# Ten sums of squares totalled by two rounded products instead of one in plain fp32

## The reference

```python
h = _rmsnorm(x, g_mix[l])                      # norm 1: over 1024
p = h @ w_in[l]
c_q = _rmsnorm(p[..., :384], g_q[l])           # norm 3: over 384
c_kv = _rmsnorm(p[..., 384:640], g_kv[l])      # norm 2: over 256
# attention from c_q, c_kv and a roped key; a gated, 31 taps wide convolution u beside it
u = silu(_layernorm(u, g_conv_ln[l], b_conv_ln[l]))   # norm 4: variance over 512
x = x + concat([y_attn, u]) @ w_o[l]
h2 = _rmsnorm(x, g_ffn[l])                     # norm 5: over 1024
z = _dwconv(h2 @ w_up[l]); zg, zv = split(z)
x = x + (silu(zg) * zv) @ w_down[l]

def _rmsnorm(x, g):
    return x * rsqrt(mean(x * x, axis=-1) + EPS) * g
```

## Time and profile before

| | |
|---|---|
| median of 3 runs | 1915.56 us (1915.34 to 1915.62) |
| the profiled execution | 1915.41 us |
| its span | 1913.5 us |
| granted TensorE clock | 1.0 of full speed |
| TensorE busy | 1881.3 us, 98% of the span, 9081 matmuls |
| VectorE busy | 1147.8 us, 60% |
| ScalarE busy | 914.6 us, 48% |
| GpSimd busy | 80.8 us, 4% |
| DMA | 171.30 MB, mean 90 GB/s |

### The profile page before, as it was taken

The page is one execution under the profiler, slowest core; times in us unless marked ns, Lnnn a source line. Parts: engine busy times, 40 slices in busy tenths (PEclk is TensorE's granted clock), DMA queues, the critical chain, the costliest instruction groups (busy, mean ns, idle before and its releaser), DMA issues.

```text
span 1913.5 us, 27153 instructions
## 1 busy us (share of the span) xinstructions
PE 1881.3 (98%) x9081; PEld 1512.6 (79%) x9081; DVE 1147.8 (60%) x1954; ACT 914.6 (48%) x1675; POOL 80.8 (4%) x116
## 2 busy tenths in 40 slices
PE   8999999899999999999999999999999999999998
PEld 6888878788888877667888888888857888888887
DVE  6777675733333366677676667436568666666534
ACT  5666673534433344556543344334466554344433
POOL 2111000000000000100100000000010020000000
PEclk9999999999999999999999999999999999999999
DMA  4222223133333323530233332333541123333333
GB/s 146 74 66 71 78 80 108 61 110 99 94 99 97 95 67 86 121 67 29 83 100 103 94 99 91 102 99 86 120 86 45 56 80 108 99 94 93 96 96 104
DMA packets 169191, 171.30 MB, mean 90 GB/s; under 512 B 48546, under 2 KB 123280, under 8 KB 169104
## 3 DMA queue, kind: packets, MB, share of 16 engines
q1 hardware_dynamic: 169000, 170.14, 31.0%
q10 hardware_dynamic: 104, 0.03, 0.0%
HBM read 159.24 MB, written 2.10 MB: 84 GB/s over the span
## 4 chain that ended last, share of the span: by engine, by line
PE 87%; DVE 8%; ACT 3%; issue 1%; DMA 0%; SPq 0%; DVEq 0%; ACTq 0%
PE bank_b L2386 15%; PE bank_b L2388 15%; PE bank_b L2387 15%; PE bank_a L2386 12%; PE bank_a L2388 11%; PE bank_a L2387 11%; PE bank_b L2860 2%; PE bank_b L2963 1%; PE bank_a L2944 1%; DVE w_lo L1508 1%; DVE arena L1511 1%; DVE arena L1508 1%; DVE h_lo L1511 1%; DVE x_t L1508 1%; PE bank_a L2860 1%
## 5 line engine op out<-in xcount | busy, mean ns | idle before, releaser
L1508 DVE TENSOR_TENSOR w_lo<-w_raw,w_hi 128x512 fp32r<-128x512 f32 (+3 forms) x621 | 413.9, 679 | 572.3 <-ACT w_hi L1225 364.5
L1225 ACT ACTIVATE w_hi<-w_raw 128x512 fp32r<-128x512 f32 (+3 forms) x396 | 233.3, 599 | 437.6 <-PE bank_b L2388 224.8
L2386 PE MATMUL bank_b<-h_hi,w_hi 128*128 128x512 f32 (+1 forms) x952 | 373.7, 393 | 8.3 <-DVE w_lo L1508 6.7
L2388 PE MATMUL bank_b<-h_hi,w_lo 128*128 128x512 f32 (+1 forms) x952 | 369.3, 388 | 0.0
L2387 PE MATMUL bank_b<-h_lo,w_hi 128*128 128x512 f32 (+1 forms) x952 | 369.2, 388 | 0.0
L864 ACT ACTIVATE w_hi<-w_raw 128x512 fp32r<-128x512 f32 x225 | 137.5, 627 | 227.1 <-PE bank_b L2388 117.7
L2386 PE MATMUL bank_a<-h_hi,w_hi 128*128 128x512 f32 (+1 forms) x600 | 233.5, 389 | 3.9 <-DVE h_lo L1511 3.6
L2387 PE MATMUL bank_a<-h_lo,w_hi 128*128 128x512 f32 (+1 forms) x600 | 232.0, 387 | 0.0
L2388 PE MATMUL bank_a<-h_hi,w_lo 128*128 128x512 f32 (+1 forms) x600 | 231.9, 387 | 0.0
L2386 PEld LDWEIGHTS bank_b<-h_hi,w_hi 128*128 128x128 f32 x952 | 178.9, 188 | 49.5 <-DVE w_lo L1508 9.5
L2387 PEld LDWEIGHTS bank_b<-h_lo,w_hi 128*128 128x128 f32 x952 | 178.9, 188 | 36.7 <-issue 1.4
(11 more groups left out here) (294 smaller groups left out, 2557.7 us busy)
## 6 DMA issues: line engine op xcount, KB each, us to landing
w_raw<-in_w_up_dram SPq DMA_DIRECT2D x240, 256.0 KB, 3.1
w_raw<-in_w_down_dram SPq DMA_DIRECT2D x152, 256.0 KB, 2.6
arena<-arena SPq DMA_DIRECT2D x32, 268.0 KB, 4.0
w_raw<-in_w_in_dram SPq DMA_DIRECT2D x64, 128.0 KB, 2.3
w_raw<-in_w_gate_dram SPq DMA_DIRECT2D x32, 256.0 KB, 2.8
w_raw<-in_w_in_dram SPq DMA_DIRECT2D x32, 256.0 KB, 2.6
w_raw<-in_w_o_dram SPq DMA_DIRECT2D x32, 256.0 KB, 2.6
w_raw<-in_w_out_dram SPq DMA_DIRECT2D x16, 256.0 KB, 2.8
```

Of the source, the lines that this page charges most:

```text
L1225: nc.scalar.activation(w_hi[:, s, 0:c], w_raw[:, s, 0:c], ACT.Copy).then_inc(w_round, 1)
L1508: return nc.vector.tensor_tensor(out_, a, b, op)
L2386: nc.tensor.matmul(out_, a_hi, b_hi, start=start, stop=False, skip_group_check=loose)
L2388: return nc.tensor.matmul(out_, a_lo, b_hi, start=False, stop=stop, skip_group_check=loose)
```

## The change

The ten totals T1 to T5 of both layers are done otherwise. When the sum is complete, VectorE copies `ssum` into a rounded tile, and subtracts that from `ssum` into a second one (`split_sum`). TensorE multiplies both by `tri[:, 1, :]` and lets PSUM add them (`split_total`). The matrix holds minus ones, so the total comes with its sign turned, and the widths that divide it are negative. The two rounded tiles `ssum_r` take no room of their own: they lie over `var` and `rs0`. `ADDS` counts the additions with the two new steps per norm. The totals of the first block stay as they were.

```diff
+ADDS = [sum(tiles + 1 for tiles in (KT, KVT, QT, HT, KT)[:n]) for n in range(6)]
...
-    "sq_ready": (3 * KT, 2 * KT + QT + KVT + HT), "sq_added": (3 * (KT - 1) - 1, 2 * KT + QT + KVT + HT - 5),
+    "sq_ready": (3 * KT, 2 * KT + QT + KVT + HT), "sq_added": (3 * (KT - 1) - 1, ADDS[-1]),
...
         ssum = sb("ssum", [P, S])
+        with nc.sbuf_tensor("ssum_r", [P, 2, S], F32R) as ssum_r:
+            pass
         var = sb("var", [P, S])
         rs0 = sb("rs0", [P, S])
...
+            def split_sum(added):
+
+                dve.wait_ge(sq_added, added)
+                nc.vector.tensor_copy(ssum_r[:, 0, :], ssum[:, :]).then_inc(sq_added, 1)
+                dve.wait_ge(sq_added, added + 1)
+                rest(ssum_r[:, 1, :], ssum[:, :], ssum_r[:, 0, :]).then_inc(sq_added, 1)
...
# T1, before the memsets of the convolution's edges
+                split_sum(added0 + ADDS[1] - 2)
                 nc.vector.memset(upad[:, :, 0:HALO], 0.0).then_inc(pad_zero, 1)
...
-                rstd_of(norm0 + 1, bank_b[:, 3, :], 1)
+                rstd_of(norm0 + 1, bank_b[:, 3, :], 1, -D)
...
# T2, behind two products of the roped key
                 tt(rot[first, 1, :], krf[second, :], trig[second, :], ALU.mult).then_inc(kr_step, 1)
+                split_sum(added0 + ADDS[2] - 2)
                 split2_lo(M_Q + 4)
...
# T3
                     add_square(t, sq0 + KT + KVT, added0 + ADDS[2], was["stat_ready"] + 2)
+                split_sum(added0 + ADDS[3] - 2)
                 split2_lo(M_PAIR + 2)
...
# T4
                     add_square(j, sq0 + KT + KVT + QT, added0 + ADDS[3], norm0 + 3)
+                split_sum(added0 + ADDS[4] - 2)
                 for k in range(5, 8):
                     split2_lo(M_WO + k)
...
# T5
                 for k in range(KT):
                     split2_lo(M_UP + SLOTS + k)
+                    if k == 5:
+                        split_sum(added0 + ADDS[5] - 2)
...
+            def split_total(bank, added):
+
+                pe.wait_ge(sq_added, added)
+                nc.tensor.matmul(bank, tri[:, 1, :], ssum_r[:, 0, :], start=True, stop=False)
+                nc.tensor.matmul(bank, tri[:, 1, :], ssum_r[:, 1, :], start=False, stop=True).then_inc(stat_ready, 1)
...
-                            total(bank_b[:, 3, :], added0 + KT - 1)
+                            split_total(bank_b[:, 3, :], added0 + ADDS[1])
```

More of the change, by code:

```diff
@@ L832, in _ @@
                 sq0, added0 = was["sq_ready"], was["sq_added"]
-                pool.wait_ge(sq_added, added0 + KT - 1)
+                pool.wait_ge(sq_added, added0 + ADDS[1])
                 def diagonals(j):
@@ L846, in _ @@
                 diagonals(0)
-                add_squares(KVT, sq0 + KT, added0 + KT - 1, was["stat_ready"] + 1)
+                add_squares(KVT, sq0 + KT, added0 + ADDS[1], was["stat_ready"] + 1)
                 diagonals(1)
@@ L851, in _ @@
                 pool.wait_ge(stat_ready, was["stat_ready"] + 4)
-                add_squares(KT, sq0 + KT + KVT + QT + HT, added0 + KT + KVT + QT + HT - 4, was["stat_ready"] + 4)
+                add_squares(KT, sq0 + KT + KVT + QT + HT, added0 + ADDS[4], was["stat_ready"] + 4)
         @block.scalar
@@ L1271, in _ @@
                 for t in range(KVT):
-                    square(bank_a[:, t, :], t, sq0 + KT, added0 + KT - 1)
+                    square(bank_a[:, t, :], t, sq0 + KT, added0 + ADDS[1])
                 split2(M_Q + 4)
@@ L1317, in _ @@
                 split2(M_PAIR + 1)
-                act.wait_ge(sq_added, added0 + KT - 1 + KVT - 1)
+                act.wait_ge(sq_added, added0 + ADDS[1] + KVT - 1)
                 for t in range(QT):
                     act.wait_ge(lat_ready, was[lat_ready.name] + KVT + t + 1)
-                    square(bank_b[:, t, :], t, sq0 + KT + KVT, added0 + KT + KVT - 2)
+                    square(bank_b[:, t, :], t, sq0 + KT + KVT, added0 + ADDS[2])
                 split2(M_PAIR + 2)
@@ L1400, in _ @@
                     act.wait_ge(dev_ready, was[dev_ready.name] + j + 1)
-                    square(conv[:, j, :], j, sq0 + KT + KVT + QT, added0 + KT + KVT + QT - 3)
+                    square(conv[:, j, :], j, sq0 + KT + KVT + QT, added0 + ADDS[3])
                 for k in range(5, 8):
@@ L1427, in input_square @@
                 def input_square(turn):
-                    square(x_t[:, UP_ORDER[turn], :], turn, sq0 + KT + KVT + QT + HT, added0 + KT + KVT + QT + HT - 4)
+                    square(x_t[:, UP_ORDER[turn], :], turn, sq0 + KT + KVT + QT + HT, added0 + ADDS[4])
                 input_hi(0)
@@ L2151, in key_behind @@
                     rest(kr_lo[ND:P, :], rot[ND:P, 0, :], kr_hi[ND:P, :]).then_inc(kr_ready, 1)
-                rstd_after(norm0 + 2, bank_a[:, 3, :], KVL, key_behind)
+                rstd_after(norm0 + 2, bank_a[:, 3, :], -KVL, key_behind)
                 for t in range(KVT):
@@ L2170, in _ @@
                 for t in range(1, QT):
-                    add_square(t, sq0 + KT + KVT, added0 + KT + KVT - 2, was["stat_ready"] + 2)
+                    add_square(t, sq0 + KT + KVT, added0 + ADDS[2], was["stat_ready"] + 2)
+                split_sum(added0 + ADDS[3] - 2)
                 split2_lo(M_PAIR + 2)
                 split2_lo(M_PAIR + 3)
-                rstd_after(norm0 + 3, bank_b[:, 3, :], QL)
+                rstd_after(norm0 + 3, bank_b[:, 3, :], -QL)
                 tt(trig_q[0], trig[:, :], rstd[:, 0, :], ALU.mult).then_inc(trig_made, 1)
@@ L2271, in _ @@
                 for j in range(HT):
-                    add_square(j, sq0 + KT + KVT + QT, added0 + KT + KVT + QT - 3, norm0 + 3)
+                    add_square(j, sq0 + KT + KVT + QT, added0 + ADDS[3], norm0 + 3)
+                split_sum(added0 + ADDS[4] - 2)
                 for k in range(5, 8):
                     split2_lo(M_WO + k)
-                rstd_into(norm0 + 4, bank_b[:, 2, :], HALF)
+                rstd_into(norm0 + 4, bank_b[:, 2, :], -HALF)
                 for j in range(HT):
@@ L2334, in _ @@
                     split2_lo(M_UP + SLOTS + k)
-                rstd_of(norm0 + 5, bank_a[:, 3, :], 1)
+                    if k == 5:
+                        split_sum(added0 + ADDS[5] - 2)
+                rstd_of(norm0 + 5, bank_a[:, 3, :], 1, -D)
                 dve.wait_ge(rstd_ready, norm0 + 5)
@@ L2878, in _ @@
                     if k == 1:
-                        total(bank_a[:, 3, :], added0 + KT - 1 + KVT - 1)
+                        split_total(bank_a[:, 3, :], added0 + ADDS[2])
                 pe.wait_ge(lat_ready, was[lat_ready.name] + KVT)
@@ L2915, in _ @@
                 keys(0)
-                total(bank_b[:, 3, :], added0 + KT - 1 + KVT - 1 + QT - 1)
+                split_total(bank_b[:, 3, :], added0 + ADDS[3])
                 for k in range(QT):
@@ L3018, in _ @@
                     if n == M_WO + HT:
-                        total(bank_b[:, 2, :], added0 + KT + KVT + QT + HT - 4)
+                        split_total(bank_b[:, 2, :], added0 + ADDS[4])
                         pe.wait_ge(dev_ready, was[dev_ready.name] + HT)
@@ L3039, in _ @@
                 pe.wait_ge(x_new, was["x_new"] + KT)
-                total(bank_a[:, 3, :], added0 + KT + KVT + QT + HT - 4 + KT - 1)
+                split_total(bank_a[:, 3, :], added0 + ADDS[5])
                 with pe.Fori(0, F2G // 2 - 1) as i:
```

## The result

The changed kernel took 1918.81 us, the median of 21 runs (1918.31 to 1920.16), against 1915.56 of the kernel before (21 runs, 1915.16 to 1916.31): a ratio of 1.0017, 95% interval 1.0011 to 1.0023. Predicted were 1918.5 us and a ratio of 1.0015. So the kernel is slower by 3.25 us, 0.17%, and the interval doesn't hold 1. The profiled execution took 1918.56 us, its span 1916.8 (before: 1915.41 and 1913.5).

A forecast was written before the change was run, and what follows sets the result against it. TensorE was taken to bound the kernel, with 87% of the span in the chain that ended last. The terms +1.18 + 1.57 + 1.57 - 3 x 0.42 = +3.06 us on 1915.41 gave 1918.5 us, range 1916.8 to 1920.6.

The forecast's parts named there:

- T5: Total behind the first up-projection block, both layers: split covered, TensorE arrives 0.42 earlier and waits 0.42 longer, so 0.
- T1.0: Layer 0's total after the first norm's sums; predicted +1.18 us.
- T4: Total in the output projection, both layers: split covered by VectorE's idle time, -0.42 us each.
- T1 of layer 0: After the first norm's sums: second wait, for the variance, ends 1.18 later and swallows the 0.42 saved; +1.18 us.
- T2 and T3: Totals in the latents' projection and after the first keys: together +1.57 us per layer, the first's cost contained in it.
- three covered totals: After layer 1's first norm's sums and in both output projections: split covered by VectorE's idle time, -0.42 us each.
- slack of 0.16: Normed conv output behind the output projection's total: of 0.58 us slack before TensorE needs its first remainder, 0.16 remains, just enough.
- Single rate copy: Rival: VectorE's copy takes 0.68 us as from PSUM, on the path five times; +1.3, 1919.8 us; chance 0.20.
- no cheaper products: Rival: a total's two rounded products cost no less than the plain fp32 one; +2.1, 1920.6 us; chance 0.05.
- Given back in the attention: Rival: TensorE's waits for ScalarE's exponentials absorb up to 1.5 us of the lateness; 1917.0 us; chance 0.08.
- No wait: Rival: VectorE reaches the split earlier, so TensorE does not wait at T2 and T3; -1.8, 1913.6 us; chance 0.04.
- Cheap waits: Rival: VectorE's chained waits cost nothing, each split 0.24 shorter, five times; -1.2, 1917.3 us; chance 0.07.

The follow-up runs named there:

- second series: The changed kernel run once more, unaltered, for comparison on the same chip with the one whose wait is filled with unread products: 1919.03 us (1918.28 to 1920.32).
- the products alone: Against the changed kernel: no splits or waits for them, two rounded products of a ready tile, variance a constant; 1913.91 us, ratio 0.9992 to the kernel before.
- the split alone: Against the changed kernel: all ten splits kept, but each total one plain fp32 product of the unsplit sum; 1920.96 us, 5.25 above before.
- the total taken later: Against the changed kernel: TensorE takes the total in the latents' projection one chunk later, behind the third chunk; 1918.80 us, 3.06 above before.

## Why the prediction was right

- **The sum.** +3.06 predicted against the profiled time, +2.91 in the profile from T1.0 to the end, +3.25 between the medians (3.26 in the second series). The forecast time was 0.3 us low. The threshold of 0.2% that the prediction set for a change that can be told from none was too coarse: with 21 runs of each the interval is 0.0006 to each side, 1.2 us.
- **The price of the parts.** Copy 0.42 against 0.425, subtraction 0.69 against 0.692, the plain total 0.88 and the pair 0.45: in the changed kernel's T4, 915.03 to 915.96, four steps of 0.23.
- **T1 of layer 0.** +1.18 against 1.17, and the saving swallowed by the variance: the products alone (-0.01) and the split alone (1.13) both show it.
- **T2 and T3.** 1.57 a layer against 1.48 and 1.50. The chain by VectorE, that the wait at T3 contains that at T2, is shown by the total taken later. The 0.1 too much is for the most part in the split's own price: I let the next operation start after the subtraction's end (1.18), but a next operation that waits for nothing begins 0.61 after its start; VectorE's place behind the split at T2 moved by 1.06. From start to start the waits at T2 were 1.83 and 1.54, where 1.82 and 1.53 were foretold. Those at T3 were 0.57 and 0.70, "about 0.7" foretold; but the prediction's own sum gives 0.37 for layer 0 (1.88 less 1.51) and 0.66 for layer 1 (1.88 less 1.22). In layer 0 TensorE came earlier than that sum has it: a short wait that the kernel before has 1.5 us ahead of the total (its product of 793.30 stands 0.41 behind the one ahead of it instead of 0.23) went away with the lateness. The time of T3 did not change by that, since VectorE ends the wait.
- **The three covered totals.** -0.42 each predicted, -0.42, -0.46 and -0.38 measured. The slack of 0.16 behind T4.0 was in truth overdrawn by 0.06 (the step of 0.28 above).
- **T5.** 0 predicted; +0.08 and -0.06, and the experiment with it plain agrees. I had the wait at the second remainder (982.81 before); 0.3 of the 0.42 was already given back at the first one, 3 us earlier.
- **Rivals.** "Single rate copy" fell with the 425 ns, "no cheaper products" with the split alone (which costs 2.0 more, the size of the five savings). "Given back in the attention" fell with the table: between T3.0 and T4.0, and between T3.1 and T4.1, there is no step but T4's own saving. "No wait" fell with 1.83. "Cheap waits" fell in its form: between copy and subtraction the wait is there, 0.46 from start to start at 0.43 of work. A piece of it was right, the overlap after the pair, 0.1 us each time. The Trainium skill (VectorE: DVE Perf Modes, The DRAIN you can't avoid) says, of eight chained copies, that a semaphore "costs nothing extra here". It does not hold for the 128x512 operations with two sources in this kernel: 0.72 start to start with a wait, 0.60 to 0.61 without.

## What to carry to other kernels

A cheaper product on the busiest engine pays only where no other engine's chain ends a wait behind it; here at five of ten places. The work that makes it cheaper costs nothing where the other engine has time for it (T4, T5 and T1 of layer 1), and counts in full where that engine's chain ends the next wait (T1 of layer 0, T2 and T3), whether the wait shows at this product or some chunks later. Place by place is the way: the same edit at five totals, two of them called a little later, gained 2.0 us, where at all ten it lost 3.3.

## What was not expected of the hardware

After a TensorE wait of 1.9 us (2.3 from the start of the last product to the next) the granted clock was 0.50 for 3.4 us, that is 1.2 GHz, in two of six executions profiled; in the other four it stayed at 1.00, that is 2.4 GHz. It fell 0.2 us behind the end of the wait in the one and 1.2 us behind it in the other. TensorE had worked without a recorded wait in the microseconds before. The kernel before, with a wait of 0.72 us at the same place, shows 1.00. What decides between the two was not found.
